# Products of constants on TensorE during the three inner norms of a hybrid encoder

## The reference

```
for l in range(2):
    h = rms_norm(x, mix_pre_norm[l]);  proj = h @ w_in[l]          # 1024 x 1952
    ... Hyena, GQA and MLA head groups on columns of proj ...
    x = x + rms_norm(groups @ w_out[l], mix_post_norm[l])          # 1024 x 1024
    h = rms_norm(x, ffn_pre_norm[l])
    up = dwconv3(h @ w_up[l], ffn_conv_w[l], ffn_conv_b[l])        # 1024 x 5632
    gate, val = split(up);  f = (gelu(gate) * val) @ w_down[l]     # 2816 x 1024
    x = x + rms_norm(f, ffn_post_norm[l])

rms_norm(x, g) = x * rsqrt(mean(x * x) + 1e-6) * g
```

## Time and profile before

| | us |
|---|---|
| median of 3 runs | 1533.15 (1531.94 to 1534.32) |
| profiled execution | 1532.87 |
| its span | 1531.1 |
| TensorE busy (matmul) | 1421.0 |
| VectorE busy | 941.8 |
| ScalarE busy | 610.8 |
| GpSimd busy | 521.7 |

### The profile page before, as it was taken

The page is one execution under the profiler, slowest core; times in us unless marked ns, Lnnn a source line. Parts: engine busy times, 40 slices in busy tenths (PEclk is TensorE's granted clock), DMA queues, the critical chain, the costliest instruction groups (busy, mean ns, idle before and its releaser), DMA issues.

```text
span 1531.1 us, 14930 instructions
## 1 busy us (share of the span) xinstructions
PE 1421.0 (93%) x5759; PEld 1050.3 (69%) x5759; DVE 941.8 (62%) x1037; ACT 610.8 (40%) x867; POOL 521.7 (34%) x239
## 2 busy tenths in 40 slices
PE   5999789988999999999979988898989999999997
PEld 3677546556688888878746765554757888887885
DVE  4766867564688787711176776666466778784112
ACT  4422345653534444332242223556335334443222
POOL 2322311014544444444452222100354444444444
PEclk8999989999899999999989999999989999999997
DMA  7211100002133333323341210000113333333231
GB/s 240 79 42 42 58 18 1 1 23 88 55 94 89 94 97 97 93 86 91 89 137 50 61 48 28 14 1 1 55 55 96 97 91 89 96 97 89 89 100 65
DMA packets 195167, 108.52 MB, mean 71 GB/s; under 512 B 5895, under 2 KB 193657, under 8 KB 194202
## 3 DMA queue, kind: packets, MB, share of 16 engines
q1 hardware_dynamic: 195098, 107.58, 23.8%
HBM read 105.47 MB, written 2.10 MB: 70 GB/s over the span
## 4 chain that ended last, share of the span: by engine, by line
PE 75%; DVE 14%; ACT 5%; issue 3%; POOL 2%; DMA 1%; DVEq 0%; POOLq 0%; SPq 0%; ACTq 0%
PE ps L877 19%; PE ps L878 19%; PE ps L879 19%; PE ps L1161 3%; PE ps L945 2%; PE ps L971 2%; PE ps L984 2%; DVE nm L1439 2%; ACT prob L700 1%; DVE p L1362 1%; POOL xT L418 1%; PE ps L1141 1%; ACT rr L481 1%; PE ps L887 1%; DVE tb L1278 1%
## 5 line engine op out<-in xcount | busy, mean ns | idle before, releaser
L411 POOL TENSOR_TENSOR wl<-raw,wh 128x1024 fp32r<-128x1024 f32 x184 | 450.6, 2450 | 877.7 <-ACT wh L470 877.7
L470 ACT ACTIVATE wh<-raw 128x1024 fp32r<-128x1024 f32 x184 | 194.8, 1059 | 611.7 <-PE ps L879 594.7
L877 PE MATMUL ps<-gh,wh 128*128 128x512 f32 (+1 forms) x896 | 366.1, 409 | 2.8 <-POOL wl L411 2.8
L878 PE MATMUL ps<-gl,wh 128*128 128x512 f32 (+1 forms) x896 | 355.7, 397 | 0.0
L879 PE MATMUL ps<-gh,wl 128*128 128x512 f32 (+1 forms) x896 | 355.2, 396 | 0.0
L877 PEld LDWEIGHTS ps<-gh,wh 128*128 128x128 f32 (+1 forms) x896 | 167.8, 187 | 51.3 <-issue 9.8
L878 PEld LDWEIGHTS ps<-gl,wh 128*128 128x128 f32 (+1 forms) x896 | 167.6, 187 | 47.1 <-issue 6.6
L879 PEld LDWEIGHTS ps<-gh,wl 128*128 128x128 f32 (+1 forms) x896 | 167.4, 187 | 43.0 <-issue 1.3
L1654 DVE SCALAR_TENSOR_TENSOR cv<-pad,pm,cv 128x512 f32<-128x512 f32 x88 | 130.4, 1482 | 84.3 <-ACT cv L779 84.3
L1262 DVE TENSOR_TENSOR acc<-acc,sq 128x512 f32<-128x512 f32 x24 | 60.6, 2525 | 195.7 <-ACT sq L514 195.5
L877 PE MATMUL ps<-fh,wh 128*128 128x512 f32 x352 | 139.2, 395 | 3.2 <-POOL wl L411 3.2
(11 more groups left out here) (225 smaller groups left out, 1953.0 us busy)
## 6 DMA issues: line engine op xcount, KB each, us to landing
raw<-w_up SPq DMA_DIRECT2D x88, 512.0 KB, 3.8
raw<-w_down SPq DMA_DIRECT2D x32, 512.0 KB, 3.6
raw<-w_in SPq DMA_DIRECT2D x30, 512.0 KB, 3.9
raw<-w_out SPq DMA_DIRECT2D x16, 512.0 KB, 3.5
raw<-w_down SPq DMA_DIRECT2D x16, 384.0 KB, 3.1
xio<-x SPq DMA_DIRECT2D x4, 512.0 KB, 4.2
win<-c_win SPq DMA_DIRECT2D x2, 1024.0 KB, 5.0
TF<-c_tf SPq DMA_DIRECT2D x2, 1024.0 KB, 8.9
```

The costliest lines, as they stand in the source:

```text
L411: nc.gpsimd.tensor_tensor(wl[:, slot, :], raw[:, slot, :], wh[:, slot, :].bitcast(F32), ALU.subtract).then_inc(S["lo_ready"], 1)
L470: A(wh[:, slot, :], raw[:, slot, :], ACT.Copy).then_inc(S["hi_ready"], 1)
L877: mm(ps[0:cols, bank, :], w_hi, x_hi, start=start and k == 0, stop=False)
L878: mm(ps[0:cols, bank, :], w_hi, x_lo, start=False, stop=False)
```

## The change

After `stat_post` at each of the three inner norms TensorE issues seven identical matmuls, `ident` by the first 512 columns of `w3`, in plain float32, into a bank that nothing reads before it is written again: bank 1 at b = 0, bank 3 at b = 1. They wait for nothing and raise no semaphore. After the last norm they are left out.

```diff
         LAG = 4
+        SPARE_BANK = [1, 3]
+        KEEP = 7
...
+            def keep_busy(b):
+
+                for _ in range(KEEP):
+                    mm(ps[:, SPARE_BANK[b], :], ident[:], w3[:, 0, 0:T], start=True, stop=True)
...
                 stat_post(lay, 0)
+                keep_busy(0)
...
                 stat_post(lay, 1)
+                if lay < DEPTH - 1:
+                    keep_busy(1)
```

## The result

The changed kernel takes 1536.08 us (median of 22 runs, 1533.29 to 1538.72), the kernel before 1533.28 us (22 runs, 1531.94 to 1535.42): 2.8 us more, ratio 1.0018 with a 95% interval of 1.0012 to 1.0025. It is slower, by a little less than the 0.2% that the prediction set as its bound, and 0.08 us outside the range. The forecast of no change was wrong; what happened is the rival "late fall", which had 11%.

The account below looks back on a forecast made before the run. TensorE, busy 93% of the span, was taken to bound the kernel, with gl setting starts after the norms. Terms 0 + 0 + 0 on 1532.87 us, plus 0.28 us to the runs' median, gave 1533.1 us; range 1530.5 to 1536.0.

Parts of the forecast that it names:

- forecast of no change: Nothing changes in the path through the three inner norms: 1533.1 us, given 83%.
- late fall: Rival: clock held over the norm's wait, then lost, low from chunk 4 on; 1534.5 to 1540 us, 11%.
- part 1: Seven products at each norm take 6.0 us, end 0.7 us before the first chunk, and cost 0.
- part 2: At the norms, nothing waits for the spare bank; engines beside the products slow by 0, at most 0.3 us a norm.
- part 3: Full clock for the norms' first triples gains 0.0 us, since gl bounds later starts; at most 0.2 us in all.
- rival of 1522 us: Each microsecond at half speed after the three norms lies on the path, so 11.1 us are gained; 4%.
- part 4: Clock may fall in the thin work after the norms' products; bounds 0 and 2.8 us, taken as 0.
- covering of norm 2: After norm 2 ScalarE's conversion waits for w_in's transfer until 788.33 us, so a late fall there costs nothing.
- price of 1.4 us a norm: A fall on chunks 4 to 7: 4.03 us of half speed lose 2.0 us, less 0.6 us of waiting for gl.
- upper end from 1535.9: The time if the late fall came at both norms where it counts, 1 and 3.

Follow-up runs that it names:

- e4: The changed kernel plus further products of the same constants after chunks 0 to 3 at all three norms: ratio 1.0005 to the kernel before.
- e16: The same kernel as e4, run once more: ratio 1.0012 to the kernel before.
- e5: The changed kernel itself, run again: ratio 1.0014 to the kernel before.
- filled kernel: The kernel of e4 and e16, with products at all three norms and in the gaps between chunks behind them: 1.0005 and 1.0012 to the kernel before.
- e12: e4 with LAG = 1 in place of 4, its filling after chunk 0 alone: ratio 1.0027 to the kernel before.
- e7: The changed kernel with one more product of the constants in layer 0 before w_out's last six column tiles: ratio 1.0016 to the kernel before.
- e8: The changed kernel with two more products of the constants in layer 0 before w_out's last six column tiles: ratio 1.0014 to the kernel before.

## Why the prediction was wrong

- *The products fit the wait and cost nothing there* (part 1): right, 0.61 us to spare where 0.7 was computed. *The bank and the ports* (part 2): right; e4's norms take 16.26 us with yet more products.
- *Full speed at the norms is worth nothing, since gl sets every start* (part 3): right, as long as the clock is back before the second slot matters. It rested on three norms with different returns of the clock; e4 and e16 show it with no half speed at all. The rival of 1522 us is refuted for the norms.
- *The late fall* (part 4) is the step that failed: a term that the sum took at 0. Mechanism, place, price and covering of norm 2 were there, and I gave it 11%. The price of 1.4 us a norm, measured 1.35 to 1.37, is partly luck: it took a fall at chunk 4 with 4.03 us of half speed, and in norm 3 half speed lasted 6.8 us, of which 4.2 happened to lie behind the start of chunk 4. The row that it was chosen by, compared how much TensorE works in a stretch: 2.64 of 5.82 us and the clock stayed. But that row ends too soon. The thin work of the kernel before goes on behind it, and the clock does fall:

```profile
204.90:210.72 5.82, 2.64 (x15) 1.00 0.10 26
210.72:214.55 3.83, 1.13 (x8) 1.00 0.32 97
214.55:221.38 6.83, 6.19 (x14) 0.50 0.00 0
```

  So both stretches of the earlier trace rows were followed by a fall, and neither spoke for 0. In the changed kernel TensorE worked 2.65 of 4.82 us, a greater share than 2.64 of 5.82, and the clock fell at once. The share over a stretch of my choice doesn't tell; the same thin work has its fall early or late from one execution to another (norm 3 of the changed kernel and of e5). With both outcomes near, the value should have been between the bounds and the rival at a half or more.
- *Not in the sum at all*: the second payment at 905 to 975 us, 0.9 to 1.6 us, when the work there is shifted against the clock. It lifts the upper end from 1535.9 to about 1537, and the range's top was too low by that. Nor was the wait for w_in's transfer after norm 2, which was 1.43 us longer in the changed kernel's profile.
- The two profiles are 4.5 us apart (spans of 1535.6 and 1531.1): 1.35 us for the late fall at norm 3; 3.0 us from norm 2 to 3, of which 1.43 are the later transfer and the rest the second payment. The 2.8 us between the medians mix executions: late fall at norms 1 and 3, 0 to 1.37 us each, and the second payment. Open is what share the later transfer after norm 2 has, and why half of the executions of the filled kernel have more low clock elsewhere and so make it measure 1.0005 and 1.0012.

The Trainium skill, TensorE: Matmul & The Clock Gate, section HAM oscillation — how this bites in real kernels, tells of bursts parted by waits of 3 to 5 us that lose the clock again and again. The 6.60 us of wait in the kernel before are that case. Norm 3 of the changed kernel is not: the clock was at 0.50 from 1139.60 us, though no gap between its triples was longer than 1.42 us. By its section Terms the price of low clock is about the throttled time times (1 - K/N), K/N being its name for the granted clock. Low clock within the span fell from 104.8 to 92.2 us, so an estimate by that page is a gain of 6.3 us; the profiled execution took 4.5 us more.

## What to carry to other kernels

Before you pay to keep TensorE's clock up over a wait, look at what follows the wait. If its operands come one by one from a slower engine, half speed is hidden, and holding the clock can move the fall to later, denser work; if dense work follows, about half of its time at half speed is lost (1.5 of 3.4 us before w_out's third tile), and a few products of constants in the wait, short enough to end before it does, bring it back (10.8 us here from three waits a layer). A row that is to show that the clock stays must be read on to the next dense work. When several executions of a kernel can lie differently against the clock, one profile is one sample: ask for the price in each position, not for what the profile happened to show.

## What was not expected of the hardware

- The clock's changes don't follow the work smoothly. The clock first reached 1.00 at 11.8 to 17.3 us, fell, and came back at 32.3 to 35.6 us in the 18 profiles. Counted from that return, the fall behind the wait in w_in (where no products stood in it) came 126.3 us later in 15 profiles, though the work of w_in ahead of it moved by up to 0.9 us between them, and 129.7 us later in e12, where that work came 2 us or more later.
- The same wait and the same work behind it can end a fall early or late: in norm 3 the clock was back at 7.4 us (e5) or at 11.6 us (the changed kernel) after the first product. Where the fall starts doesn't settle it: at norm 2 of e7 and e8 the clock fell at 3.8 us in both, and was back at 7.2 and at 10.7 us.
- Products with the identity, nearly all of whose entries are zero, are work enough to hold the clock: 1.00 over 377.00 to 383.78 us, where without them it fell at 381.8 us.
